# A Strassen-like output product with another order of block products, and the norm of half the tokens moved into it

## What is computed

```
h = layer_norm(ALPHA * h + mixer(h), ln_mix_g, ln_mix_b)
f = (silu(gate) * up) @ w_out        # gate, up = split(h @ w_in), hidden width 2816
h = layer_norm(ALPHA * h + f, ln_ffn_g, ln_ffn_b)
```

## Time and profile before

| | us |
|---|---|
| median of three runs | 2687.13 |
| the profiled execution | 2692.61 |
| its span | 2690.8 |
| TensorE busy (matmul) | 2502.1 |
| VectorE busy | 1915.3 |
| ScalarE busy | 907.9 |
| GpSimd busy | 722.4 |

### The profile page before, as it was taken

How to read it: one execution, slowest core, us unless ns; L and a number is a source line. 1 busy time by engine, 2 the same in 40 slices (tenths; PEclk the granted TensorE clock), 3 DMA queues, 4 the chain that set the end, 5 groups by cost and what they waited for, 6 DMA issues and landing times. The chain is left out here.

```text
span 2690.8 us, 39853 instructions
## 1 busy us (share of the span) xinstructions
PE 2502.1 (93%) x12860; PEld 2093.0 (78%) x12860; DVE 1915.3 (71%) x3173; ACT 907.9 (34%) x1462; POOL 722.4 (27%) x518
## 2 busy tenths in 40 slices
PE   7688599999999999988999999998799999999996
PEld 5577577778888878876888888887677888887885
DVE  8879625867877758782677666677586877775778
ACT  3323224243333345333222232222214333333532
POOL 2968420243333310021111111110024333331002
PEclk8989799999999999998999999998899999999998
DMA  4233224046677677632011110100404667767763
GB/s 139 82 111 101 69 67 157 9 145 209 198 217 218 208 274 239 218 118 62 24 31 32 39 31 23 39 23 16 157 1 137 202 208 219 215 202 267 235 224 125
DMA packets 442288, 355.97 MB, mean 132 GB/s; under 512 B 30272, under 2 KB 376512, under 8 KB 438464
## 3 DMA queue, kind: packets, MB, share of 16 engines
q1 hardware_dynamic: 442176, 354.52, 42.3%
HBM read 296.31 MB, written 58.13 MB: 132 GB/s over the span
## 5 line engine op out<-in xcount | busy, mean ns | idle before, releaser
L2443 PE MATMUL ps<-aT_hi,w_hi 128*128 128x512 f32 x624 | 251.7, 403 | 4.3 <-DVE hg_q_raw L2704 2.5
L2443 PE MATMUL ps<-aT_hi,w_lo 128*128 128x512 f32 x624 | 246.5, 395 | 0.0
L2443 PE MATMUL ps<-aT_lo,w_hi 128*128 128x512 f32 x624 | 245.2, 393 | 0.0
L2415 POOL TENSOR_TENSOR w_lo<-w_raw_plain,w_hi 128x1024 fp32r<-128x1024 f32 x38 | 91.8, 2424 | 527.4 <-ACT w_hi L62 527.4
L618 PE MATMUL ps<-aT_hi,hgo_w_sets 128*128 128x512 f32 x640 | 202.8, 393 | 0.0
L618 PE MATMUL ps<-aT_hi,s5o_w_sets 128*128 128x512 f32 x640 | 202.8, 393 | 0.0
L1312 POOL TENSOR_TENSOR s5o_w_sets_plain<-s5o_w_sets_plain 128x512 f32<-128x512 f32 x80 | 111.2, 1390 | 216.6 <-DMA s5o_w_sets_plain<-in_ffn_w_in_dram 216.6
L1312 POOL TENSOR_TENSOR hgo_w_sets_plain<-hgo_w_sets_plain 128x512 f32<-128x512 f32 x80 | 111.6, 1396 | 212.1 <-DMA hgo_w_sets_plain<-in_ffn_w_in_dram 212.1
L668 PE MATMUL ps<-aT_hi 128*128 128x512 f32 x624 | 144.3, 390 | 0.0
L618 PEld LDWEIGHTS ps<-aT_hi,s5o_w_sets 128*128 128x128 f32 x640 | 120.3, 188 | 26.4
L618 PEld LDWEIGHTS ps<-aT_hi,hgo_w_sets 128*128 128x128 f32 x640 | 120.2, 188 | 26.3
(11 more groups left out here) (424 smaller groups left out, 6238.6 us busy)
## 6 DMA issues: line engine op xcount, KB each, us to landing
s5o_w_sets_plain<-in_ffn_w_in_dram SPq DMA_DIRECT2D x168, 256.0 KB, 3.3
hgo_w_sets_plain<-in_ffn_w_in_dram SPq DMA_DIRECT2D x168, 256.0 KB, 3.3
w_raw_plain<-in_hg_w_in_dram SPq DMA_DIRECT2D x40, 512.0 KB, 4.0
aT_hi_plain<-in_ffn_w_out_dram SPq DMA_DIRECT2D x68, 256.0 KB, 4.3
s5o_w_sets_plain<-in_ffn_w_in_dram SPq DMA_DIRECT2D x96, 128.0 KB, 2.8
hgo_w_sets_plain<-in_ffn_w_in_dram SPq DMA_DIRECT2D x96, 128.0 KB, 2.8
s5o_hidden<-s5o_home_plain SPq DMA_DIRECT2D x11, 1024.0 KB, 6.6
hgo_hidden<-hgo_home_plain SPq DMA_DIRECT2D x11, 1024.0 KB, 6.7
```

Of the source, the lines that this page charges most:

```text
L2415: g.tensor_tensor(w_lo[b][:, :, :], w_raw[b][:, :, :], w_hi[b][:, :, :].bitcast(F32), ALU.subtract).then_inc(E[f"w_lo_done{b}"], 1)
L2443: ins = t.matmul(ps[:, half, :], w[b][:, kk, :], x[:, kk, cols], start=(kk == 0 and q == 0), stop=(kk == KT - 1 and q == 2))
```

## The change

The order of the block products: S3*T3, which has three accumulations per tile and sums, goes from fifth to sixth place, 12*21 from sixth to fifth, so tiles 0 to 3 are complete after the fifth product. Their moments stand at n = 62 and their centres at n = 63 to 66 in VectorE's list, the rescales beside them in ScalarE's. The accumulation of the sixth product stands at n = 75, ahead of pair_sum(75). The last product's steps lie in other buffers: home 1, home 2, then the first six of RING, then home 0, w_raw0 and home 1. Step 75 lies in w_raw0, and its load waits for that accumulation. The weights of the next layer load to home 0, right after the load of step 21, and are split at n = 33. Two operations of moments are scalar_tensor_tensor in place of tensor_scalar, one of them with a constant from a tile, magic, set once.

```
-    OUT_PRODUCTS = ["11*11", "S1*T1", "S2*T2", "S4*22", "S3*T3", "12*21", "22*T4"]
+    OUT_PRODUCTS = ["11*11", "S1*T1", "S2*T2", "S4*22", "12*21", "S3*T3", "22*T4"]
-    A_PART = [0, 3, 5, 6, 4, 1, 2]
+    A_PART = [0, 3, 5, 6, 1, 4, 2]
-    B_SUM = [False, True, True, False, True, False, True]
-    ACCS_OF = [1, 2, 2, 1, 3, 1, 1]
-    STEPS, EARLY_STEPS = 7 * NG, 5
+    B_SUM = [False, True, True, False, False, True, True]
+    ACCS_OF = [1, 2, 2, 1, 1, 3, 1]
+    STEPS, EARLY_STEPS, EARLY_NORM = 7 * NG, 5, 5 * NG + 8
+                "raw": lambda a: (k.first[:, :], k.plain["w_raw0"][:, :]),
-    LAST_RING = [("home", 0), ("home", 1), ("home", 2)] + RING[6:8] + RING[0:6]
+    LAST_RING = [("home", 1), ("home", 2)] + RING[0:6] + [("home", 0), ("raw", 0), ("home", 1)]
...
@@ SyncE
-            for n in range(LAST, LAST_STEPS):
+            for n in range(LAST, 2 * NG):
                 load_pair(n)
-            for n in range(LAST_STEPS, LAST_STEPS + 3):
-                load_pair(n)
-            s.wait_ge(S["out_acc"], accs_before(5))
-            for to, of in first_weights:
-                s.dma_start(to, of).then_inc(S["next_loaded"], 16)
-            for n in range(LAST_STEPS + 3, STEPS):
+            for b, (_, of) in enumerate(first_weights):
+                s.dma_start(next_weights[:, b * D:(b + 1) * D].rearrange("p (k n) -> p k n", k=KT), of
+                            ).then_inc(S["next_loaded"], 16)
+            for n in range(2 * NG, STEPS):
+                if place_of(n) == ("home", 0) and turns:
+                    s.wait_ge(S["next_lo"], 1)
+                if place_of(n) == ("raw", 0):
+                    s.wait_ge(S["out_acc"], accs_before(6))
                 load_pair(n)
@@ ScalarE
-                if turns and n == LAST_STEPS:
+                if turns and n == 3 * NG:
                     a.wait_ge(S["next_loaded"], 16 * len(first_weights))
-                    split_hi(a, k.hi0[:, :], k.raw0[:, :]).then_inc(S["next_hi"], 1)
-            for tt in range(PAIRS):
-                rescale(tt)
+                    split_hi(a, k.hi0[:, :], next_weights[:, :]).then_inc(S["next_hi"], 1)
+                if n - EARLY_NORM in range(PAIRS):
+                    rescale(n - EARLY_NORM)
@@ VectorE, moments
-                v.tensor_scalar(var[:, two], mv[:, two, 1], LN_EPS, None, ALU.add).then_inc(chain.sem, 1)
+                v.scalar_tensor_tensor(var[:, two], mv[:, two, 1], LN_EPS, mv[:, two, 1], ALU.add, ALU.max
+                                       ).then_inc(chain.sem, 1)
...
-                v.tensor_scalar(y.bitcast(I32), x.bitcast(I32), -0.5, 1597463007.0, ALU.mult, ALU.add
-                                ).then_inc(chain.sem, 1)
+                v.scalar_tensor_tensor(y.bitcast(I32), x.bitcast(I32), -0.5, magic[:, two], ALU.mult, ALU.add
+                                       ).then_inc(chain.sem, 1)
@@ VectorE, list
+            v.memset(magic[:, :], 1597463007.0).then_inc(S["magic"], 1)
...
             for n in range(EARLY_RING, STEPS + 1):
+                if n < STEPS and place_of(n) == ("raw", 0):
+                    accumulate(5)
...
-                if n % NG == 6 and n > NG:
+                if n % NG == 6 and NG < n < LAST_STEPS:
                     accumulate(n // NG - 1)
-            moments(range(PAIRS), 2 * NT + 3 * PAIRS)
-            centre(range(PAIRS))
+                if n == EARLY_NORM - 1:
+                    moments(range(PAIRS), 2 * NT + 2 * PAIRS)
+                if n - EARLY_NORM in range(PAIRS):
+                    centre((n - EARLY_NORM,))
@@ GpSimd
-                g.tensor_tensor(k.lo0[:, :], k.raw0[:, :], k.hi0[:, :].bitcast(F32), ALU.subtract
+                g.tensor_tensor(k.lo0[:, :], next_weights[:, :], k.hi0[:, :].bitcast(F32), ALU.subtract
```

More of the change, by code:

```diff
@@ L214, in project_and_feed @@
     mv, var, rstd, tmp = sb("mv", [P, NT, 2]), sb("var", [P, NT]), sb("rstd", [P, NT]), sb("tmp", [P, NT])
+    magic = sb("magic", [P, NT])
     S = {n: k.sem(tag + "_" + n) for n in (
@@ L221, in project_and_feed @@
         "mixed_turn", "mixed_copy", "mixed_sum", "mixed_hi", "mixed_lo0", "mixed_lo",
-        "plain_sum", "plain_hi", "plain_lo", "part", "half_silu", "half_product", "next_loaded", "next_hi", "next_lo", "stored")}
+        "plain_sum", "plain_hi", "plain_lo", "part", "half_silu", "half_product", "next_loaded", "next_hi", "next_lo", "stored", "magic")}
     w_v = w_proj.rearrange("(k p) d -> p k d", p=P)
@@ L327, in project_and_feed @@
     MIXED = [("11+22", 4, 7), ("11+12", 4, 6), ("21+22", 5, 7)]
-    OUT_PRODUCTS = ["11*11", "S1*T1", "S2*T2", "S4*22", "S3*T3", "12*21", "22*T4"]
-    A_PART = [0, 3, 5, 6, 4, 1, 2]
-    B_PARTS = [((0, 0),), ((0, 0), (0, 1)), ((1, 1),), ((1, 1),), ((0, 1), (1, 1)), ((1, 0),), ((1, 0),)]
-    B_SUM = [False, True, True, False, True, False, True]
-    ACCS_OF = [1, 2, 2, 1, 3, 1, 1]
-    STEPS, EARLY_STEPS = 7 * NG, 5
+    OUT_PRODUCTS = ["11*11", "S1*T1", "S2*T2", "S4*22", "12*21", "S3*T3", "22*T4"]
+    A_PART = [0, 3, 5, 6, 1, 4, 2]
+    B_PARTS = [((0, 0),), ((0, 0), (0, 1)), ((1, 1),), ((1, 1),), ((1, 0),), ((0, 1), (1, 1)), ((1, 0),)]
+    B_SUM = [False, True, True, False, False, True, True]
+    ACCS_OF = [1, 2, 2, 1, 1, 3, 1]
+    STEPS, EARLY_STEPS, EARLY_NORM = 7 * NG, 5, 5 * NG + 8
     LAST_STEPS = STEPS - NG
@@ L337, in project_and_feed @@
     plain_homes = [k.plain[f"{tag}_home{n}"] for n in range(4)]
+    next_weights = plain_homes[0]
     first_product = k.plain["w_raw0"][:, :].rearrange("p (t c) -> p t c", t=PAIRS)
@@ L979, in moments @@
                 v.wait_ge(S["stats"], first_stat)
+                v.wait_ge(S["magic"], 1)
                 two = slice(tiles[0], tiles[-1] + 1)
@@ L1153, in accumulate @@
                             done += 1
-                    elif p in (2, 4):
+                    elif p in (2, 5):
                         v.tensor_tensor(saved, saved, new, ALU.add).then_inc(S["out_acc"], 1)
@@ L1160, in accumulate @@
                         done += 1
-                        if p == 4:
+                        if p == 5:
                             to = part(late, 0)
@@ L1166, in accumulate @@
                     else:
-                        at = {3: (early, 1), 5: (early, 0), 6: (late, 0)}[p]
+                        at = {3: (early, 1), 4: (early, 0), 6: (late, 0)}[p]
                         v.tensor_tensor(part(*at), part(*at), new, ALU.add).then_inc(S["out_acc"], 1)
```

## The result

The kernel after takes 2708.07 us (median of 6 runs, 2703.87 to 2709.78), the kernel before 2687.39 us (6 runs). The ratio is 1.0077, with a 95% interval of 1.0067 to 1.0087: 20.7 us slower. The prediction was 2703.6 us, and slower. The profiled execution took 2709.78 us, its span is 2707.9.

The account below looks back on a forecast made before the run. TensorE, busy 93% of the span, was taken as the bound, with time to win only where it waits or has finished. Terms 7.4 + 8.8 + 0.3 = 16.5 us gave 2709.1 profiled, 2703.6 as median; forecast proper 2696 to 2710, range 2684 to 2713.

Parts of the forecast that it names:

- The port wait: VectorE's feed: three centres and one later wait per layer each stand 2.14 us until GpSimd's add_bias is over.
- The list from T: VectorE's work counted from T, the sixth product's start, both layers: accumulation until 54.0, TensorE standing some 13 us to 59.4.
- The second load behind the wait: Load of step 76, behind step 75's in SyncE's queue: no wait of its own, last pair_lo at T + 62.3.
- The low clock: TensorE after its stall: three groups of three matmuls, 0.68 us each at 2.4 GHz, run at half speed.
- Rival C: Seventh product: low clock lasts over tiles 1 and 2, or DMA for steps 75, 76 takes 5.8 us: 2706 to 2714; chance 0.09.
- The tails: Ends of both layers, later behind the late feed: +8.8 us in layer 0, +7.4 us in the last layer.
- The other terms: Outside the two tails: early loads, next layer's weights and new forms at 0, memset and waits at 0.3 us.
- the new forms: L985 and L988 of moments as scalar_tensor_tensor still wait for GpSimd: 0, between a loss of 0.3 and a gain of 2.2 us.
- the memset and its wait: One memset and a wait at each function's start: 0.3 us together, between 0 and 2 x 1.2.
- the next layer's weights: Their load, issued ahead of step 22's load: 0, at most 1.6 us; the VectorE wait they cause 0, at most 4 us.

Follow-up runs that it names:

- the kernel with the whole accumulation: Kernel after with add_bias of tiles 0 to 3 held until the last pair_lo, step 75 in home 2, sixth product accumulated whole at n = 75: 2679.69 us, ratio 0.9975.
- with it split: Kernel after with late add_bias, step 75 in home 2, and tiles 6 and 7 of the sixth product accumulated behind the loop: 2682.46 us, ratio 0.9986.

## Why the prediction was right, and what was off

**The port wait** was forecast at 2.14 us four times per layer. Three centres took 3.43, 3.42 and 3.41 us and one sum 2.88 (0.68 without), so 2.14 and 2.20. It was the term that decides the sign: with it taken out of the feed the time is that of the kernel before to half a microsecond, with an interval of 2 to 3 us either way. The Trainium skill (SBUF — State Buffer, Who interferes with whom) says that a VectorE operation with two SBUF inputs contends with a GpSimd operation that reads SBUF, and that the lock is exclusive. The traces agree, with 1.28 us alone against 3.42 beside add_bias.

**The list from T** held: the accumulation begins at T + 44.1 (forecast 43.9) and ends at 54.3 (54.0), the late load lands at 57.3 (57.5), TensorE goes on at 59.2 (59.4). It stood 12.1 us, for 13 forecast. That the load landed so near its forecast is luck in part: the last write of h came 0.4 us later than forecast (T + 53.7 for 53.3), and the load then took 3.6 us from its issue to its reader, not 4.2.

**The second load behind the wait** was sized at nothing. I let sum(76) follow at once; it waited 1.05 us for its data, and the last pair_lo came at T + 63.3, not 62.3. Both loads are issued within 1.8 us after the accumulation's last write of h. In the kernel with the bias late the same wait is 0.47 us, and 0.22 with the norm back. SyncE's timeline shows what differs, first the kernel after, then the norm back:

```profile
2671.56 0.43 SPq L507 DMA_DIRECT2D hgo_home_plain<-in_ffn_w_out_dram  x1
2672.04 3.44 SPq L538 DMA_DIRECT2D out_dram<-h  x4
```

```profile
2643.31 0.43 SPq L507 DMA_DIRECT2D hgo_home_plain<-in_ffn_w_out_dram  x1
2659.13 24.46 SPq L538 DMA_DIRECT2D out_dram<-h  x8
```

In the kernel after four tiles of h are normed by then, and their stores, 512 KB each, are issued right behind the load. With the norm back they come 16 us after it, with the bias late 10 us. The load of the last row landed 5.1 us after its issue with the stores behind it, 4.2 and 4.4 us without. The prediction named these stores and gave them no price. No run takes them alone away, so they are the likely cause, not a shown one.

**The low clock** was sized at three groups. The granted clock by windows of the kernel after (stretch, its length, busy PE PEld DVE ACT POOL, PEclk, DMA):

```profile
2675.70:2681.20 5.50, 4.27 (x9) 2.84 (x10) 3.05 (x3) 1.06 (x1) 0.00 (x0) 0.50 0.82 334
2681.30:2686.40 5.10, 5.10 (x19) 4.14 (x18) 1.38 (x2) 0.00 (x0) 0.00 (x0) 0.79 0.01 3
2686.40:2690.50 4.10, 4.10 (x19) 3.38 (x18) 3.42 (x15) 0.00 (x0) 0.00 (x0) 1.00 0.00 0
```

It stood at 0.50, 1.2 GHz, through tile 0's groups as forecast, and for part of the second tile, which took 5.1 us where I had 4.4 and full speed takes 4.1. So the second load's 1.0 and this 0.7 are the 1.8 us by which each layer's tail is later than forecast (T + 75.8 for 74.0, T + 88.4 for 86.5). Rival C named just these two and was given 0.09 as a case of its own; part of it belonged in the forecast. The measured 2708.1 us lies in C's range as well as in the forecast's own, so the time alone does not tell the two apart.

**The tails** behind that were right: third and fourth tile at 4.1 us, VectorE no longer late (it idles 3.66 us ahead of the second tile's sum), one blocked operation of 1.25 us where 1.1 was allowed. From TensorE's end to the last operation 10.2 us pass where 19.0 did, so the lag of VectorE did go; but TensorE ends 18.1 us later (T + 78.2 for 60.1), and the difference is the 9.3 us.

**The other terms**: the new forms 0, shown, and with them the memset and its wait, which the kernel with the new forms alone also has; the next layer's weights 0, as GpSimd's subtraction now runs for 4.62 us at 1044.37 and TensorE shows no new wait there.

**Median and profiled execution.** The sum gave 16.5 us and the measured difference is 20.7: 3.7 are the two tails' 1.8 and 1.9, and 0.65 lies between the layers, where 0.3 was allowed for everything else. This closes to 0.2 us, closer than the traces justify: the stretch between the layers took 1416.4 to 1422.5 us in the ten traces of this case. The profiled pair differs by only 17.2, because that trace of after is 3.4 us earlier at layer 0's T, 3.1 of it before the product with w_out begins.

## What to carry to other kernels

Work moved from an engine's idle tail into its busy feed is free only until the sum of the list reaches the consumer's time; make that list to the microsecond, with what runs beside it. Moving it also moves the work of the engines behind it: here each centre cost 1.28 us of VectorE's time, and the bias that it released on GpSimd another 2.1. Holding GpSimd back by one wait was worth some 20 us, and the move only gained once the late load was gone as well.

A transfer that needs a buffer freed by a late operation puts its whole latency behind that operation, 3.6 us here; and a stall of TensorE can be dearer than its length: behind the 12.13 us the granted clock was 0.50, and three matmuls took 1.65 us for 0.84.

## What the runs showed that was not expected

The same waits do not always cost the clock. In the kernel with the whole accumulation TensorE waited 1.64, 0.76 and 0.30 us in layer 0 and 1.64, 0.77 and 0.23 us in the last layer of one execution; the granted clock stayed at full speed in the first and fell in the second:

```profile
1161.20:1165.10 3.90, 2.74 (x9) 1.65 (x10) 3.00 (x4) 1.11 (x2) 0.77 (x1) 1.00 0.00 0
...
2640.10:2644.60 4.50, 3.45 (x10) 2.13 (x11) 2.95 (x3) 1.06 (x1) 1.43 (x1) 0.78 0.00 0
```

Nor is it only operations with two inputs in SBUF that stand beside GpSimd. The old form of the moments' two operations, tensor_scalar with one input of two columns, took 2.26 us beside GpSimd, just what the new form with two inputs took; but bn_stats, and a sum with one of its inputs in PSUM, stayed at 0.68 beside it. Which one-input operations wait, these runs don't settle.

The GpSimd operation pays too, though less: add_bias took 2.73 us behind a running VectorE operation and 2.35 alone, and four in a row took 9.44 us with the accumulation whole and 10.82 with it split, where VectorE's two-input operations came between them.
